# Residual stream and layer norms of a two-layer decoder trunk, from feature-major to token-major

## The reference

```
for l in range(DEPTH):
    x = layer_norm(ALPHA * x + 0.5 * swiglu(x, ffn1_w_gu[l], ffn1_w_down[l]), ln_w[l, 0], ln_b[l, 0])
    mix = hybrid_mixer(x, positions, w_in[l], b_in[l], attn_sinks[l], ...)
    x = layer_norm(ALPHA * x + mix, ln_w[l, 1], ln_b[l, 1])
    x = layer_norm(ALPHA * x + 0.5 * swiglu(x, ffn2_w_gu[l], ffn2_w_down[l]), ln_w[l, 2], ln_b[l, 2])
```

## Time and profile before

| | |
|---|---|
| median of 3 runs | 2532.93 us (2532.1 to 2533.38) |
| profiled execution, its own time | 2533.04 us |
| its span | 2531.2 us |
| PE busy | 2502.2 us, 99% |
| DVE busy | 1131.7 us, 45% |
| ACT busy | 974.5 us, 38% |
| POOL busy | 218.0 us, 9% |
| DMA | 229.05 MB, 90 GB/s over the span |

### The profile page before, as it was taken

The page is one execution under the profiler, slowest core; times in us unless marked ns, Lnnn a source line. Parts: engine busy times, 40 slices in busy tenths (PEclk is TensorE's granted clock), DMA queues, the critical chain, the costliest instruction groups (busy, mean ns, idle before and its releaser), DMA issues.

```text
span 2531.2 us, 31119 instructions
## 1 busy us (share of the span) xinstructions
PE 2502.2 (99%) x11306; PEld 2034.1 (80%) x11306; DVE 1131.7 (45%) x1586; ACT 974.5 (38%) x1338; POOL 218.0 (9%) x136
## 2 busy tenths in 40 slices
PE   8999999999999999999999999999999999999997
PEld 7888887778888778888788888777788887888886
DVE  3333445454554753333443333544454548333335
ACT  4443224344443354442254432433444433444323
POOL 0002121000000310001200021200000004000012
PEclk9999999999999999999999999999999999999999
DMA  4233232222222222222333223232222222332232
GB/s 164 93 99 99 92 88 76 84 67 89 78 84 87 97 82 87 96 96 92 97 100 98 88 96 106 58 92 73 78 84 84 83 88 80 100 99 95 89 103 79
DMA packets 229325, 229.05 MB, mean 90 GB/s; under 512 B 9441, under 2 KB 220641, under 8 KB 229217
## 3 DMA queue, kind: packets, MB, share of 16 engines
q1 hardware_dynamic: 229216, 227.66, 28.0%
HBM read 225.53 MB, written 2.10 MB: 90 GB/s over the span
## 4 chain that ended last, share of the span: by engine, by line
PE 95%; DVE 2%; issue 2%; POOL 1%; ACT 0%; DMA 0%; DVEq 0%; POOLq 0%; SPq 0%
PE main L1355 29%; PE main L1359 29%; PE main L1356 29%; PE side L1575 1%; DVE x L985 1%; DVE xl L979 1%; POOL ln_Q L851 1%; PE side L1391 1%; PE side L1527 1%; PE side L1561 0%; PE side L1406 0%; PE main L1386 0%; PE side L1585 0%; POOL ln_S L850 0%; PE side L1495 0%
## 5 line engine op out<-in xcount | busy, mean ns | idle before, releaser
L1355 PE MATMUL main<-xh,wh 128*128 128x512 f32 x2336 | 921.4, 394 | 8.7 <-ACT xh L556 7.3
L1359 PE MATMUL main<-xl,wh 128*128 128x512 f32 x2336 | 913.7, 391 | 2.2 <-DVE xl L979 1.2
L1356 PE MATMUL main<-xh,wl 128*128 128x512 f32 x2336 | 910.7, 390 | 0.0
L877 DVE TENSOR_TENSOR wl<-raw,wh 128x1024 fp32r<-128x1024 f32 (+1 forms) x443 | 538.9, 1250 | 634.6 <-ACT wh L547 627.8
L547 ACT ACTIVATE wh<-raw 128x1024 fp32r<-128x1024 f32 (+1 forms) x443 | 431.2, 1013 | 544.9 <-PE main L1359 537.3
L1355 PEld LDWEIGHTS main<-xh,wh 128*128 128x128 f32 x2336 | 439.2, 188 | 110.5 <-issue 12.2
L1359 PEld LDWEIGHTS main<-xl,wh 128*128 128x128 f32 x2336 | 439.0, 188 | 105.9 <-DVE xl L979 13.6
L1356 PEld LDWEIGHTS main<-xh,wl 128*128 128x128 f32 x2336 | 439.3, 188 | 91.0 <-issue 1.4
L1355 PE MATMUL main<-hh,wh 128*128 128x512 f32 x704 | 273.9, 389 | 0.0
L1356 PE MATMUL main<-hh,wl 128*128 128x512 f32 x704 | 273.9, 389 | 0.0
L1359 PE MATMUL main<-hl,wh 128*128 128x512 f32 x704 | 273.9, 389 | 0.0
(11 more groups left out here) (262 smaller groups left out, 1988.6 us busy)
## 6 DMA issues: line engine op xcount, KB each, us to landing
raw<-gu SPq DMA_DIRECT2D x180, 512.0 KB, 4.3
raw<-w_in SPq DMA_DIRECT2D x104, 512.0 KB, 4.4
raw<-down SPq DMA_DIRECT2D x80, 512.0 KB, 3.6
raw<-w_branch SPq DMA_DIRECT2D x24, 512.0 KB, 4.3
raw<-w_out SPq DMA_DIRECT2D x16, 512.0 KB, 4.0
raw<-w_in SPq DMA_DIRECT2D x24, 256.0 KB, 3.2
raw<-down SPq DMA_DIRECT2D x16, 256.0 KB, 3.7
x<-xT SPq DMA_DIRECT2D x4, 512.0 KB, 6.7
```

What stands on the lines that cost most here:

```text
L877: ins = V.tensor_tensor(put(wl[slot]), get(raw[slot]), f32(put(wh[slot])), ALU.subtract)
L1355: T.matmul(out, hi, a, start=starts and k == 0, stop=False)
L1356: T.matmul(out, lo, a, start=False, stop=False)
L1359: ins = T.matmul(out, hi, b, start=False, stop=stops and k == kk - 1)
```

## The change

The residual stream becomes token-major, `xt` [128 tokens, 4 tiles, 1024 features], in the memory of `x`.

- **Down and output projections** (`to_tokens`, `rows_slab`): the stationary operand is now the 128 by 128 block of activations, the moving one a row block of 512 weights. The result is [128 tokens, 512 features]. The number of matmuls and their 512 columns stay. The first 512 features of all four tiles go to `sd`, the second 512 to `pm`. The last two slabs are walked tile by tile, so that the four tiles end one after the other.
- **Norm** (`part_of`, `stats`, `scale`, `finish`): each tile alone, on DVE. The residual add, `bn_stats` of each half, `bn_aggr`, one pass `(x - mean) * w`, one pass `* 1/deviation + b`. ACT takes the root. The ones matmuls, `keep_clock`, the centring and everything that POOL did for norms are gone. `ln_w` and `ln_b` come by DMA, spread over the partitions.
- **Way back** (`turn_tile`, `high`, `low`): PE transposes each normed tile in 8 blocks into `sd`, ACT writes `xh` from there, DVE `xl`. Two tiles are turned among the last products of the projection, the other two among the first of the next stage.
- **First two slabs of the next stage** (`first_pair`): both slabs for tokens 0 to 255, then both for tokens 256 to 511, so 192 matmuls of 256 columns where there were 96 of 512.
- The mixer reuses the memory of `xt`, so the stream is written to DRAM (`spill`) after the third slab's load and read back before the output projection.
- At the start, x comes twice: feature-major for 256 tokens, token-major for all.
- **Attention**: a step takes two heads of each of the two key heads, and the score matmuls alternate between partitions 0 to 63 and 64 to 127. Probabilities times values are 8 matmuls of 128 columns, alternating between the two halves of the output partitions, where there were 4 of 256.
- The loops over slabs and layers are written out; the rope's table is computed once. The matrices of the branches are as before.

```diff
-def stat_sums(layer, j, idle): ...
-                pe.wait_ge(squares_sum.sem, squares_sum.val(layer, j + 1))
-                add(3, ln_Q, True, False)
-                keep_clock(4)
...
+            def turn_tile(v, t):
+                if v:
+                    pe.wait_ge(z_ready.sem, NB * (v - 1) + t + 1)
...
+                for b in range(2):
+                    for c in range(4):
+                        ins = T.transpose(sd[:, 2 * (t % 2) + b, P * c:P * c + P], xt[:, t, P * (4 * b + c):P * (4 * b + c) + P],
+                                          ident)
+                    ins.then_inc(turned.sem, 1)
...
+            def first_pair(v, g, between=None, middle=None):
+                for part in range(2):
+                    tokens = slice(256 * part, 256 * part + 256)
...
+                            for m in range(2):
+                                hi, lo = W[:, k, P * m:P * m + P], L_[:, k, P * m:P * m + P]
+                                out = pm[2 * s + m][:, tokens]
+                                T.matmul(out, hi, xh[:, k, tokens], start=k == 0, stop=False)
...
+            def rows_slab(g, ps, t, rh, rl, k0, first, last, ready=None):
+                    a, b = rh(k0 + k)[:, tile], rl(k0 + k)[:, tile]
+                    T.matmul(ps, a, W[:, k, :], start=first and k == 0, stop=False)
+                    T.matmul(ps, a, L_[:, k, :], start=False, stop=False)
+                    ins = T.matmul(ps, b, W[:, k, :], start=False, stop=last and k == kk - 1)
...
+                for t in range(NB):
+                    ins = rows_slab(g, pm[t][:, :], t, rh, rl, ka, len(groups[1]) == 2, False)
...
+                    if t == 2 and L < NORMS - 1:
+                        turn_tile(L + 1, 0)
+                    ins = rows_slab(g + 1, pm[t][:, :], t, rh, rl, kb, False, True)
+                    ins.then_inc(part_done.sem if t < NB - 1 else slab_done.sem, 1)
+                    if t == 2 and L < NORMS - 1:
+                        turn_tile(L + 1, 1)
...
+            def norm_tail(L, g, left=()):
+                split(g)
...
+                for t in range(2):
+                    stats(L, t, g + 1)
+                    scale(L, t)
+                    finish(L, t)
+                if L < NORMS - 1:
+                    low(L + 1, 0)
+                stats(L, 2, g + 1)
...
-                    for j in range(4):
-                        ins = T.matmul(sd[:, j // 2, 256 * (j % 2) + P * k0:256 * (j % 2) + 256],
+                    for a in range(2):
+                        for g in range(2):
+                            half_ = slice(HD * g, HD * g + HD)
+                            ins = T.matmul(sd[:, g, 256 * a + P * k0:256 * a + 256],
```

More of the change, by code:

```diff
@@ L228, in settle @@
             def settle(self):
[L230 to L256, removed]
+                self.eng.wait_ge(self.last.sem, self.n[self.last])
+        own_act = Signal("own_act")
+        own_dve = Signal("own_dve")
+        own_pool = Signal("own_pool")
+        raw_in = [[Signal(f"raw_in{s}{h}") for h in range(2)] for s in range(2)]
         wif_in = Signal("wif_in", 16)
@@ L600, in ffn @@
[L600 to L615 removed]
+                    split_half(0, h)
@@ L905, in outputs, with split, low @@
-            def outputs(layer, j, p, done):
-                if p == 3:
-                    dve.wait_ge(seventh_ps.sem, seventh_ps.val(layer, j + 1))
+            def split(g):
+                for h in range(2):
+                    split_half(g, h)
+            def low(v, t):
+                for b in range(2):
+                    dve.wait_ge(xhi_ready.sem, 8 * v + 2 * t + b + 1)
+                    some = (slice(None), slice(4 * b, 4 * b + 4), slice(P * t, P * t + P))
+                    V.tensor_tensor(xl[some], sd[:, 2 * (t % 2) + b, :].rearrange("p (c t) -> p c t", c=4), f32(xh[some]),
+                                    ALU.subtract).then_inc(*o.up(x_ready))
@@ new lines, in start @@
+            def start():
+                for h in range(2):
+                    split_half(0, h)
+                    for i in (2 * h, 2 * h + 1):
+                        dve.wait_ge(xhi_ready.sem, i + 1)
+                        c = slice(2 * i, 2 * i + 2)
+                        V.tensor_tensor(xl[:, c, 0:256], x0[:, c, :], f32(xh[:, c, 0:256]),
+                                        ALU.subtract).then_inc(*o.up(x_ready))
+                split(1)
+                low(0, 2)
+                low(0, 3)
@@ new lines, in part_of, with first_part @@
+                V.scalar_tensor_tensor(out=some, in0=some, scalar=ALPHA, in1=ps, op0=ALU.mult,
+                                       op1=ALU.add).then_inc(*o.up(acc_free if p and t == NB - 1 else None))
+                o.settle()
+                V.bn_stats(lst[:, t, p, :], some).then_inc(*o.up())
+            def first_part(L, t, done):
+                if L % 3 == 1:
+                    dve.wait_ge(x_back[t].sem, 16 * (L // 3 + 1))
+                elif L == 0:
+                    dve.wait_ge(xt_in[t].sem, 16)
+                part_of(L, 0, t, done, sd[:, t, :])
@@ L1033, in rope @@
+                for j in range(1, 10):
+                    split(n0 + KF + j + 1)
+                    if j == 6:
+                        for t in range(NB):
+                            first_part(L, t, n0 + KF + 6)
+                norm_tail(L, n0 + S_FFN - 1)
             def rope(layer, r, t, bank):
@@ L1592, in mixer @@
             def mixer(layer):
-                for s in range(S_MIX):
-                    n = S_FFN + s
+                n1 = layer * S_LAYER + S_FFN
+                first_pair(3 * layer + 1, n1, between=lambda: gate_products(layer), middle=lambda: middle_job(layer, 1))
+                end_job(layer, 1)
+                for s in range(2, 36):
                     t, r = divmod(s - 18, 3)
```

920 lines of the change are left out of this document (402 added, 518 removed).

## The result

The changed kernel takes 2472.48 us (median of 4, 2472.36 to 2472.66), the kernel before 2533.03 us on the same chip: ratio 0.9762, 95% interval 0.9746 to 0.9777. It is 60.6 us faster. The forecast was 50 us (2483), and its range (2473 to 2503) ends 0.5 us above the result.

What follows compares the result with a forecast made beforehand. PE bounds the kernel, busy 2502 of 2531 us. From 2533.0: interior norms -27.9, start +4.0, end -15.0, attention scores -12, probabilities times values +1, giving 2483 us; range 2473 to 2503.

Steps and rivals of the forecast that it cites:

- four visits make 0.8: Transposes at each interior norm: switching PE from products and back costs 0.2 us a visit, beside 3.5 us for 32 transposes.
- The 43.7 us: Five interior norms before the change: PE time between a projection's last product and the next stage's first, counted as removable.
- 0.3 us of waiting for each norm: Interior norms after the change: PE waits 0.3 us each for DVE's tiles, 5 x 0.3 in the sum.
- The 0.6 us for `xl`: Program start: the first products also wait for `xl`, a further 0.6 us within the start's +4.0.
- the slow stretch: Program start until 12.5 us: matmuls start 0.43 apart at PE's 1.2 GHz; claimed to depend on time and stay.
- The +1 us for the values: Attention, probabilities times values: same columns in twice as many instructions, +1 us over 16 blocks.
- the half width at 0.113: First two slabs: lower bound for a 256-column product if the fixed 0.013 us scales too, so no cost; 0.120 taken.
- the tail at 7: Program end behind the last product: lower bound 7 us, upper 11, with 8.1 taken in place of 23.1.
- rival D: Half-width products go at the weight load's pace, 0.068 us more each: +78, 2561 us, slower; chance 0.07.
- rival B: Attention scores on two row halves don't overlap, everything else as forecast: 2495 us; chance 0.13.
- VectorE's calendar: DVE's timed list at each norm: tile 3 ready at T+27.3, PE wants it at T+28; everything just in time.
- Rival C: DVE is late at the norms, 2 to 4 us for each: 2491 to 2501 us; chance 0.19.

## Why the prediction came out as it did

**The step that failed** is "four visits make 0.8", the 0.2 us of switching charged beside each turn's 0.87. There is no such cost: the 0.87 is eight transposes of 0.109 each and nothing else, so the turns take 4 x 0.87 = 3.5 and not 4.3 at each norm, 4.1 us less over the five. That visits cost nothing is shown by the split turns (+0.15 us for 12), and the transposes' own price by the doubled ones. The 0.2 was read, from start to start, at the edges of another block and added to a length of the chain. A turn has such an edge too: the second product behind it comes 0.21 behind the first and not 0.12. But the first starts 0.79 behind the turn, 0.08 before the eight transposes' 0.87 are over, and the two cancel.

**A term of the removed work was mis-sized.** The 43.7 us of the earlier trace rows came from windows of which two began where PE was busy again, and not where the next product could have started. Windows of the kernel before from that point:

```profile
369.40:377.77 8.37, 8.37 (x45) 6.23 (x44) 6.95 (x14) 3.40 (x7) 2.77 (x2) 1.00 0.00 0
882.55:892.07 9.52, 8.79 (x45) 6.63 (x46) 7.59 (x15) 3.49 (x6) 2.85 (x2) 1.00 0.32 108
...
sum 45.68, PE 42.82 PEld 31.94 DVE 37.54 ACT 18.30 POOL 15.51; mean PE 8.56 PEld 6.39 DVE 7.51 ACT 3.66 POOL 3.10
```

In the second PE is busy 8.79 of 9.52 us: the window has to hold the wait too. That is 2.0 us more than the 43.7.

**"0.3 us of waiting for each norm"** did not come: no wait of PE at a norm, 1.5 us. These three make 7.6 of the 7.9 us; 0.3 stay unplaced. At the start the same two visits' switching is up to 0.4. The 0.6 us for `xl` were 0.15 (the first product starts at 7.44 against 7.29), and the slow stretch did not stay: products are back at full pace by 11.98 and not by 12.52, about 0.4. These three cover the 1.1; they were read from the traces, not tried one by one. The first two products at full pace:

```profile
11.98 0.28 PE L1282 MATMUL main<-xh,wh 128*128 128x256 f32 x1
12.11 0.28 PE L1283 MATMUL main<-xh,wl 128*128 128x256 f32 x1
```

The +1 us for the values (0.9 too much) was a charge for more instructions that no row supported; sixteen take what eight took.

**Why the range missed.** Each of these charges was small, all were put on the same side, and none had zero as its lower bound in the range; the low edge knew only the half width at 0.113 and the tail at 7.

**What held.** The pace of products with moving weights (0.227). Half width: 0.120, as taken, with neither end of its bounds reached; rival D is out. The Trainium skill ("TensorE: Matmul & The Clock Gate", Part 3, What overlaps and what doesn't) has loads overlap only where the row groups differ; here all products use the same 128 rows, each with its own load, and the 0.120 us between starts are not the 0.213 that the prediction worked out for loads that don't overlap: the trace disagrees. Scores: -12 forecast, -12.1 in the traces, -11.7 alone; rival B is out. On this the Trainium skill ("TensorEngine Tiling (Array Packing)", Key Properties) was right, and the trace agrees: eight rows in 1.06 us on two row tiles, 1.92 on one. The tail: 8.1 forecast, 7.7 measured. VectorE's calendar: the prediction had tile 3 just in time, and it is, with 0.35 us to spare. Rival C did not occur, but one extra pass of 1.28 us is enough to start it: 0.80 to 1.06 of its 1.28 us come through at each norm.

**Where the gain comes from, shown.** Not from the layout by itself: with the same layout, same instructions and another order of the last two slabs, 46.9 of the 60.6 us are gone; with full-width pairs 59.9. Not all of that is cover: 29.4 and 46.4 us are waits, some 10 and 16 us are the slower clock behind them. The two overlap and don't add up. The norm's chain through VectorE is still 27 us long, from tile 0's last product to tile 3's last pass. It has been laid under products that don't need its result, and the order and the halves are what lays it there.

## What to carry to other kernels

When the engine that bounds a kernel waits for a chain on another, look for an order in which the pieces of that chain become ready one by one, and start the next stage on the pieces that are there, even with narrower instructions: the halves cost 1.3 us a norm, and without them a norm took 12 us more. Then measure the slack with an idle pass on the other engine; here it was 0.35 us, and whatever the next edit adds to VectorE's list beyond that is paid at each of the five norms. And a length in the chain is the whole price: don't add an edge read from starts beside it, and give each small charge zero as one of its ends.

## What the runs showed of the hardware

- A wait costs more than its length. Behind waits of 9 us for each norm a dozen products started 0.43 us apart and not 0.23; with 3.6 us of waiting in 10 the granted clock of the stretch was 0.83. At the first norm of the kernel before, idle matmuls prevent that (1.00 against 0.76 in the 6 us behind the norm), but where the next stage waits again it is worth nothing (2532.35 us without them, 2532.63 with).
- A float32 transpose of 128 by 128 costs 0.109 us in a run of eight or sixteen, and the switch from products and back costs nothing measurable (+0.15 us for 12 more visits).
- Score products of two row halves overlap even when they are issued in groups, two of one half and then two of the other (1.07 against 1.06 us).
- A product of 512 columns costs 0.23 us with 8 or with 16 stationary columns; merging two into one was paid in full, less the cost of adding the results.
